# Around the expert loop of a mixture layer: fp32 router chain, early fetch of rows, p projection moved forward, last gate block by token tiles

## Chip, cores, metric

The kernel runs on one core of one Trainium2 chip. The metric is the device time of one launch in microseconds. Timed three times, the kernel before took 1843.94 us in the median (1843.38 to 1845.05).

## What is computed

256 tokens of width 1024, all in fp32. A first block (sparse attention with three branches) is untouched by the change. The second block has two layers, and the change lies in the second layer, from its output projection on:

```
h = h + mixed @ w_o                                   # (256, 1024)
f = rmsnorm(h, ffn_norm_g)
logits = f @ router_w                                 # (256, 8)
top_vals, top_idx = top_k(logits, 2)
gates = softmax(top_vals)
h = h + sum_e combine[:, e] * (silu(f @ w1[e]) * (f @ w3[e])) @ w2[e]   # 8 experts, inner width 3584
gate = sigmoid(rmsnorm(h, ple_norm_g) @ ple_gate_w)   # (256,1024) @ (1024,1024)
h = h + gate * (p @ ple_proj_w)                       # (256,256) @ (256,1024)
```

## The kernel before

**Weights.** All weights are laid out in units of 128 x 2048 fp32 words (1 MB: four k tiles of 512 columns). SyncE (`round_loads`, `load`) fetches them in the order of use into six `raw` buffers. fp32 products are made of rounded words (fp32r): ScalarE rounds a unit to its high part `whi` (`split_to`, L621), VectorE makes the low part `wlo = raw - whi` (L961), in halves of 1024 columns, into three buffers each, two units ahead of TensorE. A product of a k tile then is three matmuls of 512 columns: high x high, low x high (L1552, L1553) and high x low (L1557). Activations are turned by TensorE (`turn_rows`, L1535), split by ScalarE into `xh` with the norm's gain (`turned_high`, L637) and by VectorE into `xl` (`turned_low`, L972). The norm's factor per token (1/rms) is applied behind the products.

**Order.** Each engine runs its own queue in the order in which it is written, and semaphores tie them together. There is no planner.

**Router.** After `mix(1)`, whose last projection has two halves (`project(2)`, `project(3)`) that VectorE adds to h (`add_part`, L1342), h is turned and split like any activation. The router's weights are split too (`rws`). 32 fp32r products of 16 or 8 columns give the logits (L1988, L1990). VectorE scales them, finds the two largest by comparing all pairs (`cmpa`, `cmpb`, `sel`), and TensorE counts slots with five fp32 products (L1994 to L1998). Meanwhile VectorE makes the normed rows `tok` (L1417), ScalarE their high part `xnh`, VectorE the low part `xnl` (L1447). From the slots VectorE makes the picks of expert 0 (`make_pick`, a 0/1 matrix), TensorE gathers its tokens by 32 products of the rows with the picks (L2015, L2016), the two engines split them (`split_gathered`, L917, L1489), VectorE computes the row numbers for scattering and fetching (`make_rows`, L1467 to L1483), and the loop starts.

**Expert loop.** There are 8 rounds here, one an expert (up to 16 if an expert has over 128 tokens). GpSimd scatters the normed rows into a DRAM scratch by expert (L584), SyncE loads each next expert's rows from it. Each round leaves its output in `yo` (128 x 1024, ScalarE, L933); SyncE stores it in the next round in two halves into `y_scratch` (L502).

**Behind the loop.** The last output is stored when both halves are copied (`store`, after all six weight loads of `ple(1)`). GpSimd fetches by token, half by half, both experts' rows (`yg`, 8 indirect fetches, L591); VectorE adds them with their gates (L1518), then `ple(1)`: h is turned and split, two blocks of gate products (48 each, 12 a half unit), then two blocks of 12 products for `p @ ple_proj_w`; sigmoid on ScalarE (L664), two VectorE steps for each half of the columns (L1397, L1401), and the store of that half (L539).

The lines that set the end:

```
            for half in range(2):
                pool.wait_ge(last_stored[half], 16)
                for T in range(NT):
                    for k in range(2):
                        pool.indirect_dma_start(yg[:, k, T, half * NB:(half + 1) * NB], None,
```

## Time and profile before

| | us |
|---|---|
| median of three timed runs | 1843.94 |
| the profiled execution | 1843.26 |
| its span, first to last instruction | 1841.5 |
| expert loop, first to last product | 833.2 to 1783.1 |
| last product to end of span | 1835.7 to 1841.5 |

Mean granted clock of TensorE 0.974 of full. Busy shares: TensorE 96%, VectorE 74%, ScalarE 66%, GpSimd 1%. In all rows a time is in us from the start of the span; a bracket at the end of a timeline row gives the engine's idle time before it and whose work ended last before it started. A matmul's shown length contains its way through the array, so that matmuls of 0.39 us follow each other every 0.23. An fp32 matmul leaves two records.

### The profile page before, as it was taken

The numbers are of one execution on the slowest core, as the hardware profiler recorded it, in microseconds if no ns is written. First come the engines' busy times: TensorE is split into PE (matmuls) and PEld (weight loads), VectorE is DVE, ScalarE is ACT, GpSimd is POOL, SyncE is SP. The second block draws the span as 40 slices with busy tenths as digits, with TensorE's granted clock in tenths as the row PEclk, the third lists the DMA queues.
The fourth block names the chain that finished last, engine by engine and source line by source line (L and its number), as shares of the span: only waits on it lengthen the run. The fifth ranks groups of instructions, "written<-read, shape, count | busy, mean of one in ns | idle before, by whom it ended". The sixth has DMA issues, their size and how long they took to land.

```text
span 1841.5 us, 26253 instructions
## 1 busy us (share of the span) xinstructions
PE 1760.2 (96%) x9290; PEld 1502.9 (82%) x9290; DVE 1368.1 (74%) x1610; ACT 1215.4 (66%) x1528; POOL 22.9 (1%) x29
## 2 busy tenths in 40 slices
PE   8999978999999989989999999999999999999977
PEld 7877867989998868877888888888888888888855
DVE  4466656656665356758989899898998898989964
ACT  5555544564444355737788787887877878788763
POOL 0000000000000000001000000000000000000010
PEclk9999998999999999979999999999999999999988
DMA  9852233427845443328999999999999999999981
GB/s 332 262 177 98 81 114 120 155 98 305 348 184 207 147 170 137 138 109 323 373 372 396 351 403 383 362 406 369 379 390 354 414 369 377 390 357 407 368 306 36
DMA packets 76544, 509.54 MB, mean 277 GB/s; under 512 B 8266, under 2 KB 8394, under 8 KB 19136
## 3 DMA queue, kind: packets, MB, share of 16 engines
q1 hardware_dynamic: 70224, 484.17, 67.9%
q0 software_dynamic: 6256, 24.48, 4.4%
q8 instruction: 44, 0.72, 0.2%
q14 instruction: 20, 0.16, 0.0%
HBM read 484.51 MB, written 24.12 MB: 276 GB/s over the span
## 4 chain that ended last, share of the span: by engine, by line
PE 89%; DVE 5%; ACT 3%; issue 2%; DMA 1%; POOL 0%; POOLq 0%; ACTq 0%; DVEq 0%; SPq 0%
PE ps L1552 23%; PE ps L1553 23%; PE ps L1557 23%; PE ps L1797 4%; PE ps L1804 4%; PE ps L1798 4%; PE ps L1535 3%; DVE wlo L961 1%; DVE sg L1084 1%; ACT sg L744 1%; PE ps L1898 1%; PE ps L1619 1%; DVE xl L972 1%; ACT xh L637 1%; PE ps L1725 1%
## 5 line engine op out<-in xcount | busy, mean ns | idle before, releaser
L961 DVE TENSOR_TENSOR wlo<-raw,whi 128x1024 fp32r<-128x1024 f32 x906 | 1043.7, 1212 | 171.4 <-ACT whi L621 169.9
L621 ACT ACTIVATE whi<-raw 128x1024 fp32r<-128x1024 f32 x906 | 901.7, 1054 | 131.3 <-PE ps L1557 108.7
L1552 PE MATMUL ps<-whi,xgh 128*128 128x512 f32 x896 | 354.3, 395 | 4.6 <-ACT whi L621 4.6
L1553 PE MATMUL ps<-whi,xgl 128*128 128x512 f32 x896 | 349.6, 390 | 0.0
L1557 PE MATMUL ps<-wlo,xgh 128*128 128x512 f32 x896 | 276.8, 390 | 0.0
L1552 PE MATMUL ps<-whi,xh 128*128 128x512 f32 (+1 forms) x448 | 184.6, 413 | 23.4 <-issue 9.9
L1552 PEld LDWEIGHTS ps<-whi,xgh 128*128 128x128 f32 x896 | 168.8, 188 | 38.5 <-ACT whi L621 4.8
L1557 PEld LDWEIGHTS ps<-wlo,xgh 128*128 128x128 f32 x896 | 168.5, 188 | 35.7
L1553 PEld LDWEIGHTS ps<-whi,xgl 128*128 128x128 f32 x896 | 168.9, 188 | 33.6
L1553 PE MATMUL ps<-whi,xl 128*128 128x512 f32 (+1 forms) x448 | 179.1, 401 | 0.0
L1552 PE MATMUL ps<-whi,mTh 128*128 128x512 f32 x448 | 175.9, 393 | 0.0
L1553 PE MATMUL ps<-whi,mTl 128*128 128x512 f32 x448 | 174.4, 389 | 0.0
L1797 PE MATMUL ps<-xh,whi 128*128 128x256 f32 x640 | 157.9, 284 | 1.2 <-issue 0.7
L1798 PE MATMUL ps<-xl,whi 128*128 128x256 f32 x640 | 156.9, 283 | 0.0
L1557 PE MATMUL ps<-wlo,mTh 128*128 128x512 f32 x448 | 138.1, 389 | 0.0
L1552 PEld LDWEIGHTS ps<-whi,xh 128*128 128x128 f32 x448 | 88.3, 197 | 44.9 <-issue 22.5
L1797 PEld LDWEIGHTS ps<-xh,whi 128*128 128x128 f32 x640 | 122.7, 192 | 2.0 <-issue 1.1
L1798 PEld LDWEIGHTS ps<-xl,whi 128*128 128x128 f32 x640 | 122.8, 192 | 0.0
L1557 PE MATMUL ps<-wlo,xh 128*128 128x512 f32 (+1 forms) x448 | 121.0, 393 | 0.0
L1553 PEld LDWEIGHTS ps<-whi,xl 128*128 128x128 f32 x448 | 88.5, 198 | 17.1 <-issue 0.2
L1557 PEld LDWEIGHTS ps<-wlo,xh 128*128 128x128 f32 x448 | 86.0, 194 | 18.4
L1557 PEld LDWEIGHTS ps<-wlo,mTh 128*128 128x128 f32 x448 | 84.1, 188 | 17.7
(300 smaller groups left out, 1745.0 us busy)
## 6 DMA issues: line engine op xcount, KB each, us to landing
raw<-in_w_moe_dram SPq DMA_DIRECT2D x336, 1024.0 KB, 7.1
raw<-in_w_fixed_dram SPq DMA_DIRECT2D x112, 1024.0 KB, 5.0
tokens_scratch<-zeros POOLq DMA_DIRECT2D x1, 8704.0 KB, 44.4
y_scratch<-yo SPq DMA_DIRECT2D x18, 256.0 KB, 7.9
y_scratch<-zeros POOLq DMA_DIRECT2D x2, 2048.0 KB, 54.2
xin<-tokens_scratch SPq DMA_DIRECT2D x8, 512.0 KB, 7.4
bias_scratch<-revb POOLq DMA_DIRECT2D x1, 3072.0 KB, 38.3
bias<-bias_scratch POOLq DMA_DIRECT2D x1, 2048.0 KB, 17.1
```

Of the source, the lines that this page charges most:

```text
L621: AC(whi[:, v % SPL, c], raw[:, v % RAW, c], ACT.Copy).then_inc(high_done, 1)
L637: ins = AC(xh[:, j, :], turned_place(k, j), ACT.Copy, scale=gains[:, k, j:j + 1])
L744: ins = AC(sg[:, i % 2, r, 0:nk], sg[:, i % 2, r, 0:nk], ACT.Exp, scale=SC, bias=ast_[:, i, 1, r:r + 1], accum_out=ast_[:, i, 2, r:r + 1])
L961: V.tensor_tensor(wlo[:, v % SPL, c], raw[:, v % RAW, c], whi[:, v % SPL, c].bitcast(F32), ALU.subtract).then_inc(low_done, 1)
L972: ins = V.scalar_tensor_tensor(out=xl[:, j, :], in0=turned_place(k, j), scalar=gains[:, k, j:j + 1], in1=xh[:, j, :].bitcast(F32), op0=ALU ...
L1535: return nc.tensor.transpose(dst, src, ident if idn is None else idn)
L1552: mm(o, hi(k0 + k, T), wh[:, k, :], start=first and k == 0, stop=False)
L1553: mm(o, lo(k0 + k, T), wh[:, k, :], start=False, stop=False)
L1557: ins = mm(o, hi(k0 + k, T), wl[:, k, :], start=False, stop=last and k == nk - 1)
L1797: mm(o, w_, xh[:, kk, :], start=kk == 0 and c % 2 == 0, stop=False, skip_group_check=True)
L1798: mm(o, w_, xl[:, kk, :], start=False, stop=False, skip_group_check=True)
L1804: ins = mm(o, wl[:, k, c * P:(c + 1) * P], xh[:, kk, :], start=False, stop=kk == KD - 1, skip_group_check=True)
```

## The change

- **Router in fp32.** The turned h goes with the gain into one fp32 tile `router_x`, four column tiles by ScalarE, four by VectorE, the router's weights stay unsplit: 16 fp32 products, the first eight ahead of the transposes of h's second half, which go by token tiles. The norm's factor isn't applied to the logits but in the exponential. Squares of h are summed by halves on ScalarE as they become ready.
- **Order of work.** VectorE splits the first weight unit of the loop and the low half of p ahead of `add_part(o1 + 2)`. `p`'s high and low parts are made here, not behind the loop.
- **Selection.** Comparisons for both token tiles in one instruction; slot counts by fp32r products, the three that the slots need first. Row numbers shifted by one so that two steps fall away.
- **Gather.** The normed rows are made by ScalarE and gathered in fp32: 16 products instead of 32, in two halves, each split by itself; the first expert product waits for the first half only (the same in each round). `make_rows` goes ahead of `split_gathered(0)` on VectorE. Zeroing `yo` moves from VectorE to GpSimd.
- **Filler products** (`keep_busy`, 512 columns, results unused): 4, 5 and 3 in the router chain, 6 behind the loop.
- **First rows.** A token's lower expert is never the last one, so its rows are fetched in the last round (four fetches into `y_low`), multiplied by their gate and added to h by GpSimd. Behind the loop there are four fetches instead of eight.
- **Last stores.** Each half of the last output is stored as soon as it is copied; these stores stand ahead of the last two weight loads.
- **Last layer.** Weight order is p projection first. Its products run right behind the loop; their results are copied to `pm`. Then the gate blocks, the last one by token tiles: 24 products for tokens 0 to 127, then 24 for the others, and sigmoid, two VectorE steps and store for each.

```diff
@@ expert loop's end, SyncE
+            for half in range(2):
+                sp.wait_ge(rows_stored[half], g.at(rows_stored[half], 0))
+            sp.sem_inc(low_rows_stored, 1)
             g.post = True
             for j, unit in enumerate(after):
+                if j == 4:
+                    for half in range(2):
+                        store(half, rounds, last_stored[half])
                 load(U["ple1"] + j, unit)
-            for half in range(2):
-                store(half, rounds, last_stored[half])
...
@@ GpSimd
+            pool.wait_ge(low_rows_stored, 1)
+            for T in range(NT):
+                for half in range(2):
+                    fetch(0, T, half, y_low, low_fetched)
+            pool.wait_ge(low_fetched, 64)
+            for T in range(NT):
+                ins = pool.tensor_scalar(y_low[:, T, :], y_low[:, T, :], gk[:, 0, T:T + 1], None, ALU.mult)
+            ins.then_inc(low_scaled, 1)
+            pool.wait_ge(low_scaled, 1)
+            pool.tensor_tensor(h[:], h[:], y_low[:], ALU.add).then_inc(low_added, 1)
             for half in range(2):
                 pool.wait_ge(last_stored[half], 16)
                 for T in range(NT):
...
+                    fetch(1, T, half, y_last, y_fetched[half])
@@ ScalarE
+            def start_router(u):
+                AC(order[:], part("square")[:, 4 * P:6 * P].rearrange("p (a n) -> p a n", a=2), ACT.Copy)\
+                    .then_inc(order_set, 1)
+                split_to(u)
+                act.wait_ge(p_loaded, 32)
+                AC(p_high_1[:], pt_in[:], ACT.Copy).then_inc(ph_done, 1)
+                split_to(u + 1)
+                for half in range(2):
...
+                        ins = AC(tok[:, T, c], h[:, T, c], ACT.Square, accum_out=st[:, o:o + 1])
...
+                    for j in range(half * KU, half * KU + 2):
+                        ins = AC(router_x[:, j, :], turned_place(5, j), ACT.Copy, scale=gains[:, 5, j:j + 1])
+                    ins.then_inc(router_x_act, 1)
...
+                for T in range(NT):
+                    ins = AC(tok[:, T, :], h[:, T, :], ACT.Copy, scale=factor(T))
+                ins.then_inc(h_normed, 1)
@@ VectorE, end of mix(1)
+                    split_to(nu)
+                    dve.wait_ge(ph_done, 2)
+                    V.tensor_tensor(p_low_1[:], pt_in[:], p_high_1[:].bitcast(F32), ALU.subtract).then_inc(pl_done, 1)
+                    add_part(B["o1"] + 2)
+                    split_to(nu + 1)
+                    router_columns(0)
...
+                    add_part(B["o1"] + 3)
+                    router_columns(1)
@@ VectorE, ahead of the loop
             make_pick()
+            count_rounds()
...
-            V.memset(yo[:], 0.0).then_inc(y_copied, 2)
+            make_rows()
             split_gathered(0)
-            make_rows()
@@ VectorE, behind the loop
+            def last_ple():
+                ub, bb = U["ple1"], B["ple1"]
+                split_to(ub + 2)
+                dve.wait_ge(low_added, 1)
+                add_last(0)
+                turned_low(6, 0)
+                add_last(1)
+                split_to(ub + 3)
+                turned_low(6, 1)
+                invert_root(6)
+                split_to(ub + 5)
...
@@ TensorE
+            def keep_busy(n, u):
+                for _ in range(n):
+                    mm(ps[:, 5, :], order[:, 1, :], whi[:, u % SPL, 0:NB], start=True, stop=True)
+
+            def last_ple():
+                ub, bb = U["ple1"], B["ple1"]
+                pe.wait_ge(pl_done, 2)
+                for j in range(2):
+                    block(ub + j, bb + j, tile_of(p_high_1), tile_of(p_low_1), kt=2)
+                pe.wait_ge(high_done, g.at(high_done, 2 * (ub + 2) + 2))
+                pe.wait_ge(y_copied, g.at(y_copied, 2))
+                keep_busy(6, ub + 2)
+                turn_rows(6, 0)
+                block(ub + 2, bb + 2, *X, norm=6)
+                b = bb + 3
+                start_block(b)
+                for T in range(NT):
+                    o, rows = ps[:, pair(b) + T, :], slice(T * P, (T + 1) * P)
+                    for u in (ub + 4, ub + 5):
...
+                    ins.then_inc(gate_row, 1)
...
+            for half in range(2):
+                if half:
+                    turn_rows(5, 1)
+                    keep_busy(4, U["ffn1"])
+                pe.wait_ge(router_x_act, half + 1)
+                pe.wait_ge(router_x_dve, half + 1)
+                for k in range(half * KU, (half + 1) * KU):
+                    for T in range(NT):
+                        ins = mm(ps[:, 4, T * NE:(T + 1) * NE], router_x[:, k, T * P:(T + 1) * P], rw[:, k, :],
+                                 start=k == 0 and T == 0, stop=k == KD - 1, skip_group_check=True)
+            ins.then_inc(router_logits, 1)
+            keep_busy(5, U["ffn1"])
...
+            mm(ps[:, 1, 0:NE], order[:, 0, :], sel[:, 0, :], start=True, stop=True)
+            mm(ps[:, 1, NE:2 * NE], order[:, 0, :], sel[:, 1, :], start=True, stop=False)
+            mm(ps[:, 1, NE:2 * NE], order[:, 1, :], sel[:, 0, :], start=False, stop=True).then_inc(slots_counted, 1)
...
+            keep_busy(3, U["ffn1"])
...
+            pe.wait_ge(pick_done, 1)
+            pe.wait_ge(h_normed, 1)
+            for half in range(2):
+                for j in range(half * KU, (half + 1) * KU):
+                    for T in range(NT):
+                        ins = mm(gathered_place(j), tok[:, T, j * P:(j + 1) * P], pick[:, T, :], start=T == 0,
+                                 stop=T == 1)
                 ins.then_inc(gathered, 1)
```

## Rows read from the trace of the kernel before

**Rows 1.** The page: chain of waits by engine; one line of DMA issues.

```profile
PE 89%; DVE 5%; ACT 3%; issue 2%; DMA 1%; POOL 0%; POOLq 0%; ACTq 0%; DVEq 0%; SPq 0%
...
y_scratch<-yo SPq DMA_DIRECT2D x18, 256.0 KB, 7.9
```

**Rows 2.** Stretches: from:to, length, busy us per engine, clock, DMA share, GB/s.

```profile
675.00:680.00 5.00, 2.53 (x15) 1.72 (x13) 4.80 (x5) 0.63 (x2) 0.00 (x0) 0.98 0.55 208
680.00:685.00 5.00, 2.20 (x5) 1.82 (x6) 4.93 (x8) 2.83 (x5) 0.00 (x0) 0.50 0.00 2
810.00:812.00 2.00, 1.31 (x7) 1.32 (x7) 1.23 (x4) 1.31 (x3) 0.00 (x0) 0.50 0.78 328
833.00:837.00 4.00, 3.81 (x9) 3.03 (x10) 2.82 (x16) 1.93 (x3) 1.10 (x2) 0.52 0.00 0
1644.00:1761.00 117.00, 117.00 (x534) 96.96 (x533) 107.18 (x106) 95.27 (x106) 0.00 (x0) 1.00 0.97 379
1803.00:1809.00 6.00, 5.52 (x14) 4.26 (x15) 0.24 (x1) 0.00 (x0) 0.00 (x0) 0.50 0.01 3
```

**Rows 3.** Timeline ahead of the loop: start, length, engine, line, operation, shapes.

```profile
798.08 1.41 DVE L1342 SCALAR_TENSOR_TENSOR h<-ps,st,h 128x512 f32<-128x512 f32 x2 [2.50 <-PE ps L1557]
...
804.79 1.40 DVE L1342 SCALAR_TENSOR_TENSOR h<-ps,st,h 128x512 f32<-128x512 f32 x2
...
810.69 0.38 PE L1988 MATMUL ps<-rws,xh 128*128 128x16 f32 x1 [1.67 <-DVE xl L972]
...
814.30 0.36 DVE L1422 TENSOR_SCALAR lg<-ps,st 128x8 f32<-128x8 f32 x2 [1.31 <-PE ps L1990]
...
816.80 0.17 DVE L1440 TENSOR_SCALAR sel<-sel 128x16 f32<-128x16 f32 x1
...
820.93 0.48 DVE L1461 TENSOR_SCALAR pick<-con,slot 128x128 fp32r<-128x128 f32 x2
...
828.60 2.17 ACT L917 ACTIVATE xgh<-ps,con 128x128 fp32r<-128x128 f32 x8 [10.77 <-PE ps L2016]
...
830.80 2.16 DVE L1489 SCALAR_TENSOR_TENSOR xgl<-ps,con,xgh 128x128 fp32r<-128x128 f32 x8 [7.23 <-ACT xgh L917]
...
833.19 0.79 PE L1552 MATMUL ps<-whi,xgh 128*128 128x512 f32 x1 [4.63 <-ACT whi L621]
...
834.87 0.19 DVE L1483 TENSOR_REDUCE gk<-rowf 128x4 f32<-128x32 f32 x1
```

**Rows 4.** Timeline behind the loop.

```profile
1781.36 0.58 ACT L933 ACTIVATE yo<-ps 128x512 f32<-128x512 f32 x1
...
1783.88 0.83 SPq L502 DMA_DIRECT2D y_scratch<-yo  x2
1786.16 1.00 POOL L591 DMA_INDIRECT yg<-y_scratch,rowy  x1 [944.59 <-DMA y_scratch<-yo]
...
1803.48 0.79 PE L1552 MATMUL ps<-whi,xh 128*128 128x512 f32 x1 [4.84 <-DVE xl L972]
...
1835.79 1.23 DVE L1397 TENSOR_TENSOR pm<-ps,pg 128x1024 f32<-128x1024 f32 x1 [0.24 <-PE ps L1557]
```

**Rows 5.** Chain of waits, pieces in order of time: start, us, what.

```profile
780.70 0.88 PE ps L1898 x6
...
793.41 1.68 PE ps L1921 x16
...
1795.03 3.63 DMA yg<-y_scratch,rowy
...
1829.35 0.91 PE ps L1557 x4
```

**Rows 6.** Timelines of GpSimd, SyncE's queue and VectorE.

```profile
432.62 0.95 POOL L571 MEMSET zeros<- 128x1024 f32 x1 [40.30 <-ACT hTh L789]
...
1744.67 16.10 SPq L494 DMA_DIRECT2D raw<-in_w_moe_dram  x7
...
1765.59 18.24 DVE L961 TENSOR_TENSOR wlo<-raw,whi 128x1024 fp32r<-128x1024 f32 x16
```

More of the change, by code:

```diff
@@ L160, in part @@
             return con[:, a:a + n]
-        ident, ntri, nones, negm, stri, ones, iota = (part("square")[:, i * P:(i + 1) * P] for i in range(7))
+        ident, ntri, nones, negm, stri, ones, place_ = (part("square")[:, i * P:(i + 1) * P] for i in range(7))
         keep = stri
@@ L427, in through @@
             def through(self, b):
-                end = block_end[b] if not (self.post and b >= B["ple1"]) else U["ple1"] + ple_end[b - B["ple1"]]
+                end = block_end[b] if not (self.post and b >= B["ple1"]) else U["ple1"] + last_ple_end[b - B["ple1"]]
                 return self.at(half_used, 2 * end)
@@ L975, in turned_low, with router_columns @@
                 ins.then_inc(xl_done, 1)
+            def router_columns(half):
+                dve.wait_ge(h_turned, 10 + half - 1)
+                for j in range(half * KU + 2, (half + 1) * KU):
+                    ins = V.tensor_scalar(router_x[:, j, :], turned_place(5, j), gains[:, 5, j:j + 1], None, ALU.mult)
+                ins.then_inc(router_x_dve, 1)
             for half in range(2):
@@ L1423, in _ @@
-            step(ins)
-            for T in range(NT):
-                ins = V.scalar_tensor_tensor(out=lg[:, T], in0=ps[:, 0, (2 * T + 1) * NE:(2 * T + 2) * NE],
-                                             scalar=factor(T), in1=lg[:, T], op0=ALU.mult, op1=ALU.add)
-            step(ins)
+            step(V.tensor_copy(lg[:].rearrange("p t e -> p (t e)"), ps[:, 4, 0:NT * NE]))
             other = lg[:].unsqueeze(2).broadcast_to([P, NT, NE, NE])
             own = lg[:].unsqueeze(3).broadcast_to([P, NT, NE, NE])
-            for T in range(NT):
-                V.tensor_tensor(cmpa[:, T], other[:, T], own[:, T], ALU.is_gt)
-                ins = V.tensor_tensor(cmpb[:, T], other[:, T], own[:, T], ALU.is_equal)
@@ L1433, in _ @@
-            step(ins)
-            for T in range(NT):
-                ins = V.tensor_tensor(cmpb[:, T], cmpb[:, T], tril8.rearrange("p (a b) -> p a b", a=NE), ALU.mult)
-            step(ins)
+            lower = tril8.rearrange("p (a b) -> p a b", a=NE).unsqueeze(1).broadcast_to([P, NT, NE, NE])
+            V.tensor_tensor(cmpa[:], other, own, ALU.is_gt)
+            step(V.tensor_tensor(cmpb[:], other, own, ALU.is_equal))
+            step(V.tensor_tensor(cmpb[:], cmpb[:], lower, ALU.mult))
@@ new lines, in _ @@
+            chosen = sel[:].bitcast(F32)
+            step(V.tensor_reduce(st[:, 12:14], lg[:], AX, ALU.max))
+            V.tensor_tensor(gw[:], lg[:], st[:, 12:14].unsqueeze(2).broadcast_to([P, NT, NE]), ALU.subtract)\
+                .then_inc(logit_shift, 1)
+            dve.wait_ge(sel_done, 1)
+            dve.wait_ge(slots_counted, 1)
+            step(V.scalar_tensor_tensor(out=slot[:], in0=ps[:, 1, 0:NT * NE].rearrange("p (t e) -> p t e", t=NT),
+                                        scalar=1.0, in1=chosen, op0=ALU.add, op1=ALU.mult))
@@ L1470, in make_rows @@
                                             scalar=float(P), in1=low, op0=ALU.mult, op1=ALU.add))
-                V.scalar_tensor_tensor(out=high, in0=low, scalar=1.0, in1=sel[:], op0=ALU.add, op1=ALU.mult)
-                step(V.scalar_tensor_tensor(out=low, in0=low, scalar=float(2 * NE * P), in1=sel[:], op0=ALU.subtract,
-                                            op1=ALU.mult))
+                V.tensor_tensor(high, low, chosen, ALU.mult)
+                step(V.scalar_tensor_tensor(out=low, in0=low, scalar=float((2 * NE + 1) * P + 1), in1=chosen,
+                                            op0=ALU.subtract, op1=ALU.mult))
@@ L1512, in _ @@
             g.r = rounds
-            for half in range(2):
-                c = slice(half * NB, (half + 1) * NB)
-                dve.wait_ge(y_fetched[half], 64)
-                for k in range(2):
-                    for T in range(NT):
-                        ins = V.scalar_tensor_tensor(out=h[:, T, c], in0=yg[:, k, T, c], scalar=gk[:, k, T:T + 1],
-                                                     in1=h[:, T, c], op0=ALU.mult, op1=ALU.add)
-                    if k == 0:
-                        step(ins)
-                ins.then_inc(h_combined, 1)
-            dve.wait_ge(h_combined, 2)
             g.split = U["ffn1"] + 2
             g.post = True
-            ple(1)
+            last_ple()
         @block_.tensor
@@ L1839, in turn_hidden, with second_half @@
                     ins.then_inc(hidden_turned, 1)
+                def second_half():
+                    pe.wait_ge(gather_low, g.at(gather_low, 2))
                 for f in range(NFB):
-                    block(ub + 4 * f, bb + 2 * f, *x, nt=1)
+                    block(ub + 4 * f, bb + 2 * f, *x, nt=1, between=second_half if f == 0 else None)
                     if f:
@@ L2003, in turn_tokens @@
+            mm(ps[:, 0, 0:NE], order[:, 1, :], sel[:, 1, :], start=False, stop=True).then_inc(slots_counted, 1)
+            keep_busy(3, U["ffn1"])
             def turn_tokens():
```

356 lines of the change are left out of this document (206 added, 150 removed).

## Prediction

> **What bounds the kernel now.** I read the chain of waits first, on the page: 89% of the span is TensorE, 5% VectorE, 3% ScalarE [rows 1]. Then the table by stretches: in a round of the expert loop TensorE is busy for all 117.0 of 117 us at clock 1.00, VectorE for 107.2 [rows 2]. The change leaves the number of products in the loop alone, so the eight rounds should cost what they cost now. What is left are the stretches before and behind the loop, and there I read the timeline, looking at the brackets that name an idle time. Before the loop TensorE does no weight product from 804.3 (VectorE's last add starts behind it, at 804.79) to 833.2, and its clock is down from 810 on (0.50) and still low until about 836.8, 3.6 us into the products (0.52 in 833 to 837) [rows 2, 3]. Behind the loop the last product ends at 1783.1 and the first of the next block starts at 1803.5: store, eight indirect fetches on one queue, adds, transposes, split [rows 4].
>
> **Part 1, the router chain.** A schedule step by step, each time against the one of before.
> Start: VectorE now splits weight unit 0 (2 x 1.2 us, and ScalarE reaches it 0.4 later) and the low half of p (0.7) before its first add, which starts at 799.8 and not at 798.08 [rows 3]. TensorE is busy with the first half of its last projection until 800.5, so of the 1.7 us it sees 0.7: the last projection ends at 805.05, not 804.3.
> fp32 router: the trace has fp32 products whose moving side is narrow: 16 records (8 products) in 1.68 us, 0.21 each; and wide ones: 6 records with 512 columns in 0.88, so 0.22 for 128 columns [rows 5]. The 16 router products thus cost 3.4 us, as many as the 32 of before at full clock. Their first half (1.7) now stands ahead of the transposes of the second half: these start at 806.8 although the first add is ready at 805.8. Eight transposes 0.9, columns copied by two engines at once 0.9 to 1.0, second half 1.7: logits at 810.75, against 814.30 [rows 3]. Gained 3.5, of which about 1.7 is the second half at full clock.
> Logits to selection: 2.67 us before (814.30 to 816.97 [rows 3]); with one copy for four scalings and whole 128-element comparisons I count 1.9: 812.65.
> Selection to picks: before 4.4 us, to 821.4. In it were a 2.28 us low part of the normed rows on VectorE, five fp32 products at low clock, and seven small steps of 0.2 [rows 3]. Now three products (0.35), 0.4 until they are seen, one step 0.2, picks 0.5, some 0.2 of handoffs: 814.3. The normed rows are made by ScalarE (root 809.5, two copies of 1.07) by 811.9, which is early enough; zeroing the output tile goes to the idle GpSimd (0.95 for its like [rows 6]) and costs nothing.
> Gather: 7.1 us before (to 828.60 [rows 3]); now 16 fp32 products x 0.22 = 3.5, in halves at 816.1 and 817.9.
> Split: ScalarE's first half is ready at 817.5. But VectorE now does the rounds (0.8), the gate weights (1.0 plus handoffs) and all row numbers first; these took 2.1 (from 832.95, end of the split, to 835.06 [rows 3]) and end at about 818.3. That queue is late next, and not TensorE. First half of its split: half of 2.16, so 819.4, and the first expert product starts at 819.7, against 833.19: gained 13.5. The second half is ready at 820.5 and its unit is needed 2.7 us after the start: hidden.
> Clock: if filler products hold it, the first 3.6 us of expert products, now at half speed, cost half: another 1.7. The fillers (12 of 512 columns, 0.23 each) stand in waits for other engines and I cost them at nothing; at low clock the last three would push the gather by about 1. Part 1: **15.2 us**.
>
> **Part 2, behind the loop.**
> The lower expert's rows: SP has issued the last round's last weight load at 1760.8 (1744.67 + 16.10 [rows 6]) and then releases GpSimd. Four fetches of 1.27 each (eight issues from 1786.16 to 1795.03 [rows 4, 5]) end at 1766, land within some 8 us while the DMA engines are full (the y store takes 7.9 there [rows 1]): 1774. Then GpSimd multiplies 2 x 1024 columns and adds 2048. The trace has no GpSimd arithmetic. Lower bound: 4096 columns at the rate of its memset (0.95 per 1024 [rows 6]) are 3.8 us; upper bound three times that, 11.4, since it reads where the memset only writes. I take 7, so it is done at 1781, before the 1784.3 at which it is wanted; with the upper bound it is 1 us late.
> Does this hold up VectorE? From 1765.6 on it makes low parts back to back, 16 in the 18.24 us listed, 1.14 each, where TensorE takes 1.36 for each; it runs about 5 us ahead [rows 6]. If it stopped for the whole arithmetic, 7 us, less what it regains, some 1 us would come out at TensorE; with 11.4 about 5. I take 0.5.
> The Trainium skill, "SBUF — State Buffer", section "Who interferes with whom", says of this that a VectorE instruction with two SBUF inputs and a GpSimd instruction that reads SBUF exclude each other for the whole instruction; the split of weights is such an instruction. No run here shows it yet. By the Trainium skill, "GPSIMD Engine Reference", section "3.1 Elementwise — side-by-side cycle accounting", an add of 2048 fp32 columns takes 4.5 us on GpSimd; with 2.2 for the multiplications the sum would be 6.7, all of it taken from VectorE. This goes into the second rival.
> Last rows: the first half of the output is now stored by itself: copied by 1781.94, on its way at 1782.05; store to GpSimd took 2.3 (1783.88 to 1786.16), so 1784.3 [rows 4]. Two fetches instead of four per half: the second is issued at 1785.6 and lands 3.63 later [rows 5], 1789.2. New is that two 1 MB weight loads are now queued behind the stores and run at that time: between 0 and 4.3 (7.9 less 3.6) more; I take 1. Two adds of 0.75: h at 1791.7. From the end of such adds to the next product, over transposes, high and low parts, before the router: 806.2 to 810.69, 4.5 us [rows 3]. First gate product 1796.2, against 1803.48 [rows 4]. The second half's rows land by 1793 and are added behind the first low part: hidden.
> p projection: 24 products of 0.2275 (0.91 for four [rows 5]) = 5.5 us go into the wait, from 1783.1 to 1788.6, and fillers until 1790. What had covered them was nothing; now VectorE and ScalarE have that time too.
> Clock: after the fillers TensorE has only transposes for 6 us. The same happened at 676 to 682.8: 0.98 up to 680, then 0.50 [rows 2]. So I expect the clock to fall and the first 5.3 us to run at half speed as they do now (0.50 in 1803 to 1809 [rows 2]).
> From the first gate product to the last product of all are 32.2 us now (1803.48 to 1835.7, just ahead of VectorE's 1835.79 [rows 4]); less 5.5 is 26.7, so the end is at 1822.9. The order by token tiles changes no count: 48 products again. Weight units 4 and 5 are loaded at about 1784.5, split by 1810 and needed at 1808 to 1811, so not late by the schedule, but with little to spare.
> Behind the last product: now 5.8 us: two VectorE steps of 1.23 from 1835.79, and 3.2 from their end to the span's end at 1841.5 [rows 4]. With a tile of 128 tokens: sigmoid 0.64 and handoffs 0.3, two steps of 0.62, 0.2, and 2.6 for half the bytes: 5.0. End at 1827.9 instead of 1841.5. Part 2: **13.6 us**, less 0.5 for VectorE: 13.1.
>
> **Sum.** 15.2 + 13.1 = 28.3. The profiled execution took 1843.3 (span 1841.5 and 1.8 around it); 1843.3 - 28.3 = 1815.0. The median of the timed runs is 0.7 above it, so I say 1815.5.
>
> **Rivals.**
> A. The clock falls before the gather all the same. For it: between 805 and 810.6 only the four fillers are dense, and at 810 it fell before. Against: no stretch without dense work is longer than 2.7 us, and it held in 675 to 680 for 3.5 us without any. Then the second half of the router takes 3.4, the gather 7, the first products run slowly: the loop starts at 823.2, part 1 is worth 10.0. Time 1820.7.
> B. GpSimd and VectorE exclude each other, and the arithmetic waits for gaps or takes the upper bound. The last round loses up to 5 at TensorE, or the fetches of the last rows, queued behind the arithmetic on GpSimd, go out 3 to 5 late. Time 1820 (1818 to 1824). Against it: ten free microseconds before 1784.
> C. Better than I say: the clock survives the wait behind the loop (2.6) and the loads don't disturb the fetches (1). Time 1812. Against: 676 to 683.
> D. Slower than before. GpSimd's arithmetic is of another order. Everything of the tail waits for it: the last fetches, the adds, the gate. It starts at 1774 and has 10 us; beyond this each microsecond is one of the span. The other gains are spent when it lasts 38 us, ten times the memset's rate; at 45 us the time would be 1850. For it speaks only that the trace has no such operation.
> E. The change doesn't do what it says: the rows of the lower expert aren't ready in the last round because SP comes to its signal late, or the split chain on VectorE (rows first) holds the loop. Then each part keeps about half: 1829.
>
> **Chances.** Forecast 0.50, A 0.18, B 0.13, C 0.09, E 0.06, D 0.04. The forecast's own range is 1812.5 to 1819. For 8 in 10 I take 1810.5 to 1826: it holds A, B, most of C. About 0.2% (3.7 us) is what a measurement of this kernel can tell from no change. Faster by more 0.95, within it 0.01, slower 0.04.
>
> **What would show it.** In the profile after: first product on the gathered tokens at about 820 and clock 1.00 there; the 16 gather products 0.22 apart; GpSimd's arithmetic between 1760 and 1770 of the new span (13 to 15 us earlier than here) and no idle TensorE in the last round; first gate product some 13 us behind the loop's last product, with the p products between; last product to end 5 us. I am wrong if TensorE idles in a round, if the loads of gate units 4 and 5 end a wait, or if the gather products are 0.43 apart.

## The result and the profile after

The changed kernel takes 1829.84 us (median, 1829.60 to 1830.73); the kernel before, timed beside it, 1844.49. The ratio is 0.992, 95% interval 0.9907 to 0.9932. Faster, as predicted, but by 14.7 us instead of 28.3. The predicted time was 1815.5, and 1829.84 lies outside both the forecast's own range (to 1819) and the wider one (to 1826). The profiled span is 1828.2 us, 13.3 less than before.

Part 1 came as drawn. Timeline of the changed kernel ahead of the loop (start, length, engine, line, operation, as in [rows 3]):

```profile
803.72 1.41 DVE L1436 SCALAR_TENSOR_TENSOR h<-ps,st,h 128x512 f32<-128x512 f32 x2 [0.81 <-PE ps L1669]
...
809.32 0.17 DVE L1553 COPY lg<-ps 128x16 f32<-128x16 f32 x1 [1.43 <-PE ps L2142]
...
811.03 0.17 DVE L1563 TENSOR_SCALAR sel<-rank 128x16 fp32r<-128x16 f32 x1
...
812.16 0.48 DVE L1576 TENSOR_SCALAR pick<-con,slot 128x128 f32<-128x128 f32 x2
...
813.54 4.47 PE L2170 MATMUL ps<-pick,tok 128*128 128x128 f32 x32
...
817.45 1.13 DVE L1613 SCALAR_TENSOR_TENSOR xgl<-ps,con,xgh 128x128 fp32r<-128x128 f32 x4 [1.07 <-ACT xgh L1006]
...
818.80 0.49 PE L1664 MATMUL ps<-whi,xgh 128*128 128x512 f32 x1 [0.79 <-DVE xgl L1613]
```

Logits at 809.3 (predicted 810.75), first expert product at 818.80 (predicted 819.7, before 833.19). The first product has its full-clock duration, 0.49, where it had 0.79 [rows 3].

Part 2 did not. The last expert output is copied out at 1767.02, 16.1 us earlier than before (1783.12), yet the span is only 13.3 shorter. GpSimd's timeline behind that point, with all it did there:

```profile
1751.70 13.18 POOL L613 DMA_INDIRECT y_low<-y_scratch,rowy  x1 [929.91 <-SPq L552]
1765.18 0.97 POOL L613 DMA_INDIRECT y_low<-y_scratch,rowy  x1 [0.30 <-issue]
1766.45 0.99 POOL L613 DMA_INDIRECT y_low<-y_scratch,rowy  x1 [0.30 <-issue]
1767.74 0.95 POOL L613 DMA_INDIRECT y_low<-y_scratch,rowy  x1 [0.31 <-issue]
1775.66 5.68 POOL L624 TENSOR_SCALAR y_low<-y_low,gk 128x1024 f32<-128x1024 f32 x2 [6.97 <-DMA y_low<-y_scratch,rowy]
1781.43 4.49 POOL L627 TENSOR_TENSOR h<-h,y_low 128x2048 f32<-128x2048 f32 x1
1786.08 1.02 POOL L613 DMA_INDIRECT y_last<-y_scratch,rowy  x1 [0.15 <-issue]
```

The fetch of the last expert's rows (last line) has no wait of its own left: 0.15 idle, released by "issue", that is by its place in the queue. The store that it needs had been issued at 1766.01. The chain of waits of the changed kernel says the same, read downward in time:

```profile
1745.75 5.56 issue
1751.70 13.18 POOL y_low L613
1767.74 7.83 DMA y_low<-y_scratch,rowy
1775.66 5.68 POOL y_low L624 x2
1781.40 4.53 POOLq L140
1787.41 3.55 DMA y_last<-y_scratch,rowy
1792.52 1.99 PE ps L1647 x8
```

Before, this chain went from the last copy over store and fetch to the adds [rows 4, 5]. Now it begins in the middle of the last round and runs through GpSimd: the work meant to lie beside the loop has become the path. The stretches of the changed kernel (columns as in [rows 2]) show no wait in the last round, the clock half down during the gather, and the hole in front of the last gate blocks:

```profile
806.00:812.00 6.00, 5.08 (x33) 4.04 (x31) 3.06 (x13) 5.28 (x9) 0.95 (x1) 0.97 0.17 66
812.00:819.00 7.00, 6.21 (x38) 5.74 (x38) 4.99 (x31) 2.10 (x9) 1.77 (x2) 0.78 0.17 68
1650.00:1760.00 110.00, 110.00 (x504) 91.17 (x503) 100.92 (x101) 90.51 (x104) 8.30 (x1) 1.00 0.97 373
1774.00:1786.00 12.00, 0.00 (x0) 0.00 (x0) 0.00 (x0) 0.00 (x0) 10.18 (x3) 0.65 0.23 95
1786.00:1800.00 14.00, 3.94 (x13) 3.16 (x14) 5.28 (x9) 3.46 (x6) 3.88 (x4) 0.50 0.28 75
```

From 1774 to 1786 only GpSimd works, 10.2 of 12 us. In the first 14 us after it the clock stands at 0.50.

**The measure used below.** Kernels that share all code up to the router still reach it up to 6 us apart (the last add starts at 803.72 in the changed kernel, at 810.06 in best below), so small changes of the tail drown in the total. I therefore take the *tail* from each profile: from the start of the copy of the last rows' second half (`yo`, second of two) to the end of the span. The two starts, before and changed:

```profile
1783.12 0.60 ACT L933 ACTIVATE yo<-ps 128x512 f32<-128x512 f32 x1 [1.18 <-PE ps L1557]
```

```profile
1767.02 0.60 ACT L1021 ACTIVATE yo<-ps 128x512 f32<-128x512 f32 x1 [1.18 <-issue]
```

Before 1841.5 - 1783.12 = 58.4; changed 1828.2 - 1767.02 = 61.2. The loop itself, first expert product to that copy, is 949.9 before and 948.2 in the changed kernel (1.7 for products no longer at half the clock, as predicted). It is steady: 948.2 in all the kernels below but one (early_pool). A tail is read from one trace for each kernel. low_dve and probe, which differ only in two small GpSimd instructions, have 50.1 and 50.6, so I read nothing from a difference of half a microsecond.

### The profile page after: what moved, and what is told of

Read it like the earlier page. It is cut to its first block, busy times and chain, and to the rows that moved or that the text cites. A ratio compares the mean times of both kernels' runs of the same rounds, so it can differ in the third digit from the quotient of the medians.

```text
span 1828.2 us, 26305 instructions
## 1 busy us (share of the span) xinstructions
PE 1754.7 (96%) x9303; PEld 1497.1 (82%) x9303; DVE 1362.0 (74%) x1591; ACT 1221.8 (67%) x1533; POOL 45.4 (2%) x33
## 4 chain that ended last, share of the span: by engine, by line
PE 87%; DVE 5%; ACT 3%; issue 2%; POOL 1%; DMA 1%; POOLq 0%; SPq 0%; DVEq 0%; ACTq 0%
PE ps L1664 22%; PE ps L1665 22%; PE ps L1669 22%; PE ps L1918 4%; PE ps L1925 4%; PE ps L1919 4%; PE ps L1647 3%; DVE wlo L1049 2%; DVE sg L1178 1%; POOL y_low L613 1%; ACT sg L816 1%; PE ps L2022 1%; PE ps L1740 1%; ACT whi L658 1%; ACT xh L674 0%
## 5 line engine op out<-in xcount | busy, mean ns | idle before, releaser
L1664 PE MATMUL ps<-whi,xh 128*128 128x512 f32 (+1 forms) x432 | 177.7, 413 | 22.1 <-issue 10.0
L1665 PE MATMUL ps<-whi,xl 128*128 128x512 f32 (+1 forms) x432 | 172.1, 400 | 0.0
L1669 PE MATMUL ps<-wlo,xh 128*128 128x512 f32 (+1 forms) x432 | 116.6, 393 | 0.0
L1664 PEld LDWEIGHTS ps<-whi,mTh 128*128 128x128 f32 x448 | 84.1, 188 | 17.0
## 6 DMA issues: line engine op xcount, KB each, us to landing
bias<-bias_scratch POOLq DMA_DIRECT2D x1, 2048.0 KB, 17.4
```

The source lines that it names most:

```text
L1664: mm(o, hi(k0 + k, T), wh[:, k, :], start=first and k == 0, stop=False)
L1665: mm(o, lo(k0 + k, T), wh[:, k, :], start=False, stop=False)
L1669: ins = mm(o, hi(k0 + k, T), wl[:, k, :], start=False, stop=last and k == nk - 1)
```

## The experiments

Theory: the gain of part 2 went into a new chain on GpSimd that stands in its queue ahead of the last rows' fetches: a signal 7 us late, a first fetch 12 us too long, 10 us of arithmetic. The diffs below show each edit's main lines. Rivals: the last rows' own store and landing set the time; or part 1 was worth less than it looks and part 2 did gain.

### Part 1 alone: front_only

```diff
-        return proj + gate if i else gate + proj
+        return gate + proj
-            pool.wait_ge(low_rows_stored, 1)
...
+            for half in range(2):
+                pool.wait_ge(last_stored[half], 16)
+                for T in range(NT):
+                    for k in range(2):
+                        fetch(k, T, half, y_last if k else y_low, y_fetched[half])
```

> The changed kernel with the router part as changed, and behind the expert loop the order of the kernel before (six weight units in the old order and the stores behind them, all eight row fetches behind the stores, both experts' rows added by VectorE, gate blocks ahead of the p projection). Theory: the router part alone is worth what the profile of the changed kernel shows at the loop's end, 1783.12 to 1767.02, so 16.1 us of 1844.5: 1828.4 us. Then the whole part behind the loop gives nothing (1829.8 measured for both together, so +1.4). Rival: the router part is worth only the 14.4 us by which the first expert product came earlier, 1830.1, and the other 1.7 us in the loop belong to the new order behind it; then the part behind the loop gives about nothing too. If it is above 1833, the part behind the loop did help and the router part was worth less than its trace says.

Measured: 1827.63 us (1826.66 to 1833.03), ratio 0.9913 (0.9884 to 0.9941). Tail 1824.9 - 1767.42 = 57.5. So part 1 alone has all of the gain (18.3 us by the medians here, 16 by its trace). The intervals of the two ratios overlap, so the timed runs don't show whether part 2 gives or costs anything. By the tails of the two traces, part 2 as built costs 3.7 us (61.2 against 57.5). The rival that part 2 did gain falls. The loop takes 948.2 here too, so the 1.7 us gained in it belong to part 1, against the rival in the expectation.

### Who does the adds: low_dve

```diff
-            pool.wait_ge(low_fetched, 64)
-            for T in range(NT):
-                ins = pool.tensor_scalar(y_low[:, T, :], y_low[:, T, :], gk[:, 0, T:T + 1], None, ALU.mult)
-            ...
-            pool.tensor_tensor(h[:], h[:], y_low[:], ALU.add).then_inc(low_added, 1)
+                dve.wait_ge(low_fetched, 64)
+                for T in range(NT):
+                    ins = V.scalar_tensor_tensor(out=h[:, T, :], in0=y_low[:, T, :], scalar=gk[:, 0, T:T + 1],
+                                                 in1=h[:, T, :], op0=ALU.mult, op1=ALU.add)
```

> The changed kernel, with the low expert's rows scaled and added to h by two VectorE instructions of 1024 columns instead of GpSimd's three. Theory (the last rows' fetches queue behind GpSimd's arithmetic): GpSimd is free at 1775.7 instead of 1785.9, so the last rows' fetches and all behind them come 10.2 us earlier: 1819.6 us, and down to 1817 if TensorE's clock no longer falls in the shorter wait. The first fetch stays at 13 us, its landing at 7 to 8. Rival 1 (the arithmetic excludes VectorE and was not itself on the path): less than 2 us, 1828. Rival 2 (the last rows' store or landing sets the time): the fetches go out earlier but land only a little earlier, 1826.

Measured: 1821.02 us (1819.19 to 1822.76), ratio 0.9864 (0.9839 to 0.9889). The time expected was 1819.6. Tail 1821.0 - 1770.90 = 50.1: 11.1 us less than the changed kernel, the 10.2 of arithmetic and a bit of what follows. The two adds on VectorE take 2.48 us for what took GpSimd 10.2. GpSimd's timeline of this kernel, and VectorE's adds:

```profile
1755.33 13.42 POOL L613 DMA_INDIRECT y_low<-y_scratch,rowy  x1 [929.64 <-SPq L552]
...
1774.07 1.59 POOL L613 DMA_INDIRECT y_last<-y_scratch,rowy  x1 [1.50 <-DMA y_scratch<-yo]
...
1778.83 2.48 DVE L1521 SCALAR_TENSOR_TENSOR h<-y_low,gk,h 128x1024 f32<-128x1024 f32 x2 [3.99 <-DMA y_low<-y_scratch,rowy]
```

The first fetch is as long as ever (13.42), but the last rows' fetch now waits for its own store (1.50, "DMA y_scratch<-yo"). Both rivals said under 4 us and fall. And with the arithmetic gone, neither the late signal nor the long fetch costs much.

### The fetch in the last round: early_pool and early_dve

```diff
-            pool.wait_ge(low_rows_stored, 1)
+            for half in range(2):
+                pool.wait_ge(rows_stored[half], 16 * NE)
```

SyncE's own two waits and its signal behind the loop are dropped. early_dve has the edit of low_dve as well.

> The changed kernel, but GpSimd itself waits for the eighth store of rows (a constant that holds for the 8 rounds of this input) and not for SyncE's word at its loop's end; the arithmetic stays on GpSimd, and so falls into the last round. Theory: the late signal (7 us) and the blocked fetch (12 us) then lie beside the loop, the last rows are fetched when their store has landed, about 1769.4 instead of 1786.1: 16.7 us, 1813 us. If VectorE's gapless stream is what shut the first fetch out, that fetch lasts until VectorE has its first gap, in the last round too, and VectorE's operations run longer beside GpSimd's arithmetic (7 to 10 us of it), which TensorE may feel: up to 7 us, 1820. If it was cold code or a busy queue, the first fetch is long whatever VectorE does, or short (1 us) because the queue is quieter, and the loop is not longer. Rival: the last rows' chain is bound by something else (store, landing): over 1822.

> As early_pool, with the low expert's rows added by VectorE behind the loop (2 instructions, about 2.7 us, while the last rows are still under way). Theory: 1813 us as well, 1 to 3 us under early_pool if GpSimd's arithmetic beside the loop cost the loop anything. Rival: 1819.6, as low_dve, if only the arithmetic's place mattered and not the fetches'.

Measured: early_pool 1823.58 us (1818.50 to 1824.65), ratio 0.9883 (0.9859 to 0.9908), tail 1816.7 - 1768.27 = 48.4; early_dve 1818.60 us (1817.22 to 1819.61), ratio 0.9856 (0.9832 to 0.9880), tail 1815.4 - 1767.99 = 47.4. Both are under low_dve's tail, by 1.7 and 2.7, but not by the 6 or 7 expected. By the medians early_pool is no better than low_dve (1821.02) and early_dve only slightly, and the intervals of all three ratios overlap. The theory's 1813 us is missed by 10 and 6; the measured times lie near those of the two rivals (over 1822, and 1819.6). GpSimd's arithmetic in early_pool, beside VectorE's stream:

```profile
1657.43 1.90 POOL L610 DMA_INDIRECT y_low<-y_scratch,rowy  x1 [835.67 <-DMA y_scratch<-yo]
...
1672.56 11.94 POOL L622 TENSOR_SCALAR y_low<-y_low,gk 128x1024 f32<-128x1024 f32 x2 [8.13 <-DMA y_low<-y_scratch,rowy]
1684.59 5.46 POOL L625 TENSOR_TENSOR h<-h,y_low 128x2048 f32<-128x2048 f32 x1
```

and VectorE in that time:

```profile
1672.67 4.62 DVE L1047 TENSOR_TENSOR wlo<-raw,whi 128x1024 fp32r<-128x1024 f32 x4
...
1684.36 9.03 DVE L1047 TENSOR_TENSOR wlo<-raw,whi 128x1024 fp32r<-128x1024 f32 x4
```

17.4 us instead of 10.2, and VectorE's four splits 9.03 instead of 4.62 while GpSimd adds: each engine waits for the other. TensorE felt it once (0.91 idle at 1691, waiting for `wlo`), and the loop is 949.5, where every other kernel with the new router part has 948.2. So even hidden, this arithmetic costs 1.3 us. A first fetch after 836 us of waiting took 1.90 here, so cold code is not what made it 13.

Why not 1813? In early_dve the store and fetches go out early, the rows come late:

```profile
1769.06 0.86 SPq L514 DMA_DIRECT2D raw<-in_w_fixed_dram  x2
...
1769.22 0.95 POOL L610 DMA_INDIRECT y_last<-y_scratch,rowy  x1 [103.82 <-DMA y_scratch<-yo]
...
1778.16 1.41 DVE L1510 SCALAR_TENSOR_TENSOR h<-y_last,gk,h 128x512 f32<-128x512 f32 x2 [3.84 <-DMA y_last<-y_scratch,rowy]
```

8.9 us from first fetch to add, where the prediction has 5.9. The half's last fetch, issued at 1770.48, has 7.7 us to the add; in front_only it is 3.7 (1774.30 to 1778.02). The difference between the two is what the change queued behind the stores: two 1 MB weight loads, issued from 1769.06.

### Loads and rows: loads_first, best, rows_first

loads_first is low_dve, and best is early_dve, with the loads ahead of the stores; rows_first is early_dve with the last two loads behind the rows.

```diff
# loads_first, best
             for j, unit in enumerate(after):
-                if j == 4:
-                    for half in range(2):
-                        store(half, rounds, last_stored[half])
                 load(U["ple1"] + j, unit)
+            for half in range(2):
+                store(half, rounds, last_stored[half])
# rows_first
                         store(half, rounds, last_stored[half])
+                    sp.wait_ge(y_fetched[0], 32)
```

> low_dve with one thing put back: SyncE issues all six weight loads before the two stores of the last rows, as the kernel before did. Theory: in low_dve and early_dve two 1 MB loads went out 2.1 us after the first store (at 1771.98 and 1769.06), and the rows fetched behind them landed 6 to 7 us after their issue, against 2.8 to 3.6 us in front_only, where nothing else was under way; with the loads ahead the last rows' first half comes about 3 us earlier, so 1818 us. Rival 1: the store now goes out later than it did, because the sixth load waits for its buffer, and eats the gain: 1821 us. Rival 2: GpSimd is not ready before 1773 because of the long first fetch of the low expert's rows (13.4 us) and the three behind it, so only 1 us is left of it: 1820 us.

> early_dve (GpSimd fetches the low expert's rows in the last round, on its own wait; VectorE adds them behind the loop) with the loads ahead of the stores. Theory: the last rows are fetched at 1769.2 and land at about 1774.0 instead of 1778.1 (early_dve), so 4 us less than early_dve: 1814.5 us, and up to 2 us less again where TensorE's wait is now short enough for its clock to stay up. Rival: the landing does not depend on the two loads: 1818.5 us as early_dve.

> early_dve with the last two weight loads held back until the first half of the last rows has landed (SyncE waits for y_fetched[0]); in best the same two loads, put ahead of the stores, made the first store land 4.9 us after its issue instead of 2.2. The measure is the stretch from the start of the copy of the last rows' second half to the end of the span, since the time ahead of the expert loop differs by up to 6 us between executions that share all of that code: 58.4 us before, 61.2 in the changed kernel, 47.4 in early_dve, 46.4 in best. Theory (store, fetch and loads share the DMA engines, and the rows are what TensorE waits for): store as in early_dve, landing of the first half at about 1774.2 on its scale instead of 1778.1, first transposes 4 us earlier: 43.5 us, and 1814.5 us in all. Rival: the held loads are late for the last gate block, 47 us or more.

Measured: loads_first 1820.53 us (1820.12 to 1824.22; tail 1818.4 - 1768.77 = 49.6, low_dve 50.1); best 1820.96 us (1817.93 to 1821.54; tail 1819.7 - 1773.33 = 46.4, early_dve 47.4). Little, and not the 3 and 4 us expected. Timelines of SyncE's queue and of GpSimd in best:

```profile
1772.32 1.98 SPq L522 DMA_DIRECT2D y_scratch<-yo  x2
...
1777.24 0.95 POOL L609 DMA_INDIRECT y_last<-y_scratch,rowy  x1 [106.50 <-DMA y_scratch<-yo]
```

From store to fetch it is now 4.9 us (7.0 in loads_first, 1767.75 to 1774.71), in early_dve 2.25: the loads that no longer sit on the rows sit on the store. (The median of best is above early_dve's. In the two profiled executions that difference lies ahead of the loop, in code that both share: the products start at 825.1 instead of 819.8. For the other executions it isn't known.) rows_first takes both off: 1815.51 us (1813.68 to 1816.38), ratio 0.9833 (0.9816 to 0.9849), tail 1811.9 - 1768.54 = 43.4, expected 43.5:

```profile
1774.90 1.41 DVE L1511 SCALAR_TENSOR_TENSOR h<-y_last,gk,h 128x512 f32<-128x512 f32 x2
1776.37 0.86 PEld L1645 LDWEIGHTS ps<-con,h 128*128 128x128 f32 x8 [1.33 <-DVE h L1511]
```

The adds start 6.4 us behind the second copy instead of 10.2, with no wait for a DMA in front of them; the held loads are in time.

### What shuts the fetch out: gaps and probe

```diff
# gaps: in VectorE's split, last 16 of each round
+                            V.memset(st[:, 60:61], 0.0).then_inc(gap_made, 1)
+                            dve.wait_ge(gap_made, g.at(gap_made, 2 * w + half + 1))
# probe: on GpSimd, behind the signal
+            pool.memset(y_low[:, 0, 0:64], 1.0).then_inc(low_scaled, 1)
+            pool.wait_ge(low_scaled, 1)
+            pool.tensor_scalar(y_low[:, 1, 0:64], y_low[:, 0, 0:64], 2.0, None, ALU.mult).then_inc(low_scaled, 1)
+            pool.wait_ge(low_scaled, 2)
```

> low_dve, but in every round VectorE waits for a tiny write of its own behind each of its last 16 splits of weights, so that it stands still for a moment after each; nothing else differs, and the first fetch of the low expert's rows is issued by SyncE's word as in low_dve. Theory (the first fetch is shut out as long as VectorE goes from one instruction to the next without a gap): it now lasts 1 to 2.3 us instead of 13.4, and the four fetches end by about 1762. Rival 1 (busy queues or the weight loads make it long): still 10 us or more. Rival 2 (GpSimd's code is cold when it has waited 930 us): unchanged too, but early_pool's 1.9 us after 836 us of waiting speak against it.

> low_dve with two small GpSimd instructions between SyncE's word and the first fetch: a memset of 64 columns and a multiplication of 64 columns that reads what it wrote. Theory (GpSimd gets at SBUF only when VectorE leaves a gap): the memset or the multiplication is the long one, 10 us or more, ends about 0.1 to 0.9 us after VectorE's first gap, and the first fetch behind it takes 1 to 2 us. Rival (it is the fetch's own descriptors that are held up): both small instructions take under 0.5 us, and the fetch still lasts to VectorE's first gap, over 10 us.

Both were run once. First probe, then gaps, GpSimd's timeline behind SyncE's word:

```profile
1752.25 0.15 POOL L619 MEMSET y_low<- 128x64 f32 x1 [929.50 <-SPq L552]
1752.50 12.74 POOL L621 TENSOR_SCALAR y_low<-y_low 128x64 f32<-128x64 f32 x1
1765.51 1.67 POOL L613 DMA_INDIRECT y_low<-y_scratch,rowy  x1 [0.27 <-POOL y_low L621]
```

```profile
1757.86 1.00 POOL L614 DMA_INDIRECT y_low<-y_scratch,rowy  x1 [930.06 <-SPq L553]
1759.16 1.02 POOL L614 DMA_INDIRECT y_low<-y_scratch,rowy  x1 [0.30 <-issue]
```

Both rivals of gaps fall, busy queues and cold code, and so does that of probe. A GpSimd instruction that only writes 64 columns takes 0.15 us in the middle of VectorE's stream; one that reads 64 columns takes 12.74. So neither the fetch's queue nor its code holds it up; a plain read of SBUF by GpSimd is held up just the same. The stretches of probe up to and behind the point where it is let in show VectorE at 12.99 of 13.00 us, then with air:

```profile
1752.00:1765.00 13.00, 13.00 (x59) 10.78 (x58) 12.99 (x12) 10.96 (x11) 12.65 (x2) 1.00 0.69 245
...
1765.00:1768.00 3.00, 3.00 (x15) 2.49 (x14) 2.45 (x2) 1.55 (x2) 2.42 (x3) 1.00 0.15 14
```

With a short stop behind each split (VectorE busy 8.9 of 10 us in gaps), the same fetch at the same place takes 1.00. The Trainium skill, "SBUF — State Buffer", section "Who interferes with whom", gives the rule: a VectorE instruction with two SBUF inputs contends with a GpSimd instruction that reads SBUF, and not with one that only writes it. The trace agrees, 12.74 against 0.15. The section infers that descriptor generation needs the write side and so is left alone by such a stream; here the measurement decides otherwise, 13.18 us for an indirect fetch. That a fetch is held up because it takes its row numbers from SBUF, which is a read, is argued from these two runs and not shown by itself.

Its price is small once the arithmetic is gone: gaps has a tail of 1820.3 - 1772.99 = 47.3 (1822.15 us in all, its products starting 6 us late as in best), low_dve 50.1, so 2.8 us. That is also all that early_dve gains over low_dve: with the fetch let in, SyncE's late word costs nothing that the tails show. Each of these figures is from one run. probe took 1820.45 us (tail 50.6, as low_dve).

### Clock and token tiles: rows_fill, gate_whole, front_no_fill

```diff
# rows_fill, on rows_first
-                keep_busy(6, ub + 2)
+                keep_busy(9, ub + 2)
                 turn_rows(6, 0)
+                start_block(bb + 2)
+                for _ in range(13):
+                    mm(ps[:, pair(bb + 2), :], order[:, 1, :], whi[:, (ub + 2) % SPL, 0:NB], start=True, stop=True)
                 block(ub + 2, bb + 2, *X, norm=6)
# gate_whole, on rows_first
-                for T in range(NT):
-                    o, rows = ps[:, pair(b) + T, :], slice(T * P, (T + 1) * P)
...
+                block(ub + 4, bb + 3, *X)
```

front_no_fill is the changed kernel less `keep_busy(4, ...)`, `(5, ...)` and `(3, ...)` of the router part.

> rows_first with 9 instead of 6 matrix products without use ahead of the transposes, and 13 more behind the first transposes, where TensorE stands still for 3.5 us in every version (1781.60 in early_dve). Theory: TensorE's granted clock stays at 1.00 through the wait for h; the gate products that ran at half the clock (in early_dve the clock was 0.50 to about 1789) take half as long: 3 us less than rows_first, 40.5 us of the stretch behind the copy and 1811.5 us. Rival: the clock falls all the same, or the fillers end late and hold the gate products up: rows_first's time or up to 2 us more.

> rows_first with the last gate block as one block again (whole sigmoid, whole product and sum of 1024 columns, one output store), to price the change's work by token tiles. By the rows of before the end behind the last product is 1.0 of ScalarE, 1.2 and 1.2 of VectorE in place of 0.7, 0.7 and 0.7, so the stretch is 1.5 to 2 us longer than rows_first's. Rival: the token tiles win nothing, because the first tile's work was hidden anyway and the output store sets the end: under 0.5 us.

> The changed kernel without the 12 products without use in the router part (the 6 behind the loop stay). Measured from the last product of the output projection (803.72 in the changed kernel) to the first expert product (818.80), 15.1 us. Theory: without them the clock is at half for the gather and the logits; the 32 records of the gather take about 6.6 us instead of 4.5 and the logits and transposes a little longer, 17.5 to 18.5 us, and the first expert products up to 4 us at half the clock, so 20 us in all by the loop's end. Rival: the clock would not have fallen, 15.1 us.

rows_fill: **1811.70 us** (1810.96 to 1815.88), ratio 0.9818 (0.9799 to 0.9837), tail 1809.2 - 1768.16 = 41.0, the fastest of all and faster than both kernels (the changed one has 0.992, 0.9907 to 0.9932). The stretch behind the transposes, rows_first and then rows_fill:

```profile
1776.00:1784.00 8.00, 4.09 (x15) 3.28 (x16) 4.00 (x8) 3.57 (x6) 0.00 (x0) 0.70 0.75 310
```

```profile
1776.00:1784.00 8.00, 7.48 (x38) 6.00 (x39) 4.22 (x8) 3.58 (x6) 0.00 (x0) 1.00 0.68 284
```

Granted clock 1.00 instead of 0.70; 2.4 us of tail for 16 useless products. (Every kernel with early_dve's wait holds a constant for 8 rounds and is not general as it stands.)

gate_whole, one run, 1818.88 us: tail 1817.1 - 1771.40 = 45.7, 2.3 more than rows_first: the token tiles are worth a little more than the 1.5 to 2 expected. Storing the last output by halves and the p projection ahead of the gate have no run of their own. front_no_fill, one run, 1832.41 us: first expert product 820.18 - 803.89 = 16.3 us behind the last add instead of 15.1, last copy 1768.38, so 1.2 us later in all. I had expected 5. Stretches of front_no_fill, then of the changed kernel:

```profile
812.00:815.00 3.00, 2.37 (x10) 2.31 (x11) 1.97 (x14) 0.49 (x2) 0.00 (x0) 0.50 0.45 175
815.00:818.00 3.00, 3.00 (x16) 3.00 (x15) 2.23 (x17) 0.36 (x2) 0.00 (x0) 0.50 0.00 0
818.00:821.00 3.00, 2.85 (x19) 2.53 (x18) 1.12 (x4) 1.73 (x8) 2.34 (x3) 0.87 0.43 175
```

```profile
812.00:815.00 3.00, 3.00 (x12) 2.71 (x12) 2.62 (x17) 0.01 (x1) 0.00 (x0) 0.50 0.25 94
815.00:818.00 3.00, 3.00 (x27) 2.83 (x25) 1.79 (x14) 1.14 (x4) 1.05 (x1) 0.99 0.00 0
```

The fillers bring the clock back some 3 us sooner, within the gather. Without them the gather itself brings it back before the expert products, so these lose nothing: 1.2 us is all that the fillers of part 1 earn.

## Why the prediction was wrong

**Part 1 (predicted 15.2, measured about 16) was right**, step for step within 2 us: logits 1.4 early, first product 0.9 early, 1.7 at the head of the loop. Two details were off. VectorE's row numbers, named as "late next", were not: its split waited 1.07 us for ScalarE. And the gather took 4.5 us and not 3.5, since the clock was at 0.50 up to 815 in spite of the fillers, as rival A had it; it came back during the gather, so A's other costs did not arise.

**Part 2 (predicted 13.1, measured -2.8) failed in its first paragraph, "the lower expert's rows".** On the changed kernel's scale (16.1 us earlier) the schedule ran:

- *Last weight load issued "at 1760.8", "and then releases GpSimd"*: 1744.7 here, as planned, but the word came at 1751.70, 7.0 us late. The chain books 5.56 of it as "issue", between SyncE's branch on the number of rounds (L546, at 1745.7) and its next instruction (L551, at 1751.3). In between, at 1749.5 to 1749.8, lies one packet of the DMA queue that loads instructions; whether SyncE waited for it no run shows.
- *"Four fetches of 1.27 each"*, 5.1 us: they took 17.0, the first alone 13.18. +11.9. I did cite the rule of exclusion, but applied it to the arithmetic only: a fetch reads SBUF too.
- *Landing 8*: 7.0 from the end of the last issue. -1.0.
- *Arithmetic "I take 7"*: 10.25. +3.3. It lay inside my bounds (3.8 to 11.4), near the upper end. The add of 2048 columns took 4.49, as the 4.5 that the prediction names for it; the two multiplications took 5.68 where it had 2.2.

Together 21 us late: ready at 1785.9 instead of 1764.9, wanted at 1768.2. So the last rows' fetches went out 17.9 us late. The rest of the tail was priced well: fetch to adds 5.0 (5.9), adds to first gate product 7.0 (6.0), 25.6 to the last product (26.7), 4.6 behind it (5.0). 17.9 - 0.9 + 1.0 - 1.1 - 0.4 = 16.5 against the plan, less 1.4 (0.9 more gained in front, and the 0.5 booked for VectorE, which TensorE never lost): the 15 us that are missing.

**What decided** was less each delay than the order: the arithmetic stood in GpSimd's queue ahead of fetches that did not need it. low_dve keeps the late word and the long fetch, takes only the arithmetic away, and has 11.1 of the 16.5 back; early_dve 2.7 more. The schedule asked whether the low rows were ready in time and gave the queue behind them a sentence ("go out 3 to 5 late") in rival B. B named the mechanism, exclusion and late fetches behind the arithmetic, at 0.13 and at less than a third of its size (3 to 5 late, measured 17.9); its "ten free microseconds" were eaten before the arithmetic began. The time came out beside rival E's 1829, which had the late signal, but not as E had it: part 1 kept all and part 2 nothing.

**Two terms in part 2 were guesses that the runs now price.** The loads behind the stores: I took 1 of a range of 0 to 4.3. In the changed kernel they ran while GpSimd was busy and cost the last rows nothing; once the fetches are on time (early_dve against rows_first) they cost 4.0. "The clock will fall behind the fillers" was right (0.50 in 1786 to 1800); holding it is worth 2.4, near the 2.6 of rival C.

## What to carry to other kernels

Work moved off the path onto an idle engine must be followed to what stands behind it in that engine's queue; if something urgent does, the moved work is on the path again, with all its delays. GpSimd is idle but not free: while VectorE streams instructions with two SBUF inputs, a GpSimd instruction that reads SBUF, and a fetch with row numbers too, can wait for a gap (12.74 and 13.18 us here), and VectorE in turn can wait for GpSimd (9.03 instead of 4.62). Where a small transfer ends the path, keep large loads off the DMA engines both ahead of its store and behind it; give the loads a wait on the rows.

## What the runs showed of the hardware

- A GpSimd instruction (a fetch, in probe a read of 64 columns) was shut out beyond the end of the current VectorE instruction: in the changed kernel over ten such ends in a row, 1.135 us apart. It took 12.74 to 13.74 us in four kernels (changed, low_dve, loads_first, probe; 13.18, 13.42, 13.74, 12.74), and 1.00 with a stop behind each. In early_pool, with VectorE also going from one split to the next, a fetch came through in 1.90. What tells these two apart stays open; no run was made for it.
- Both sides pay: GpSimd's multiplications 11.94 instead of 5.68, its add 5.46 instead of 4.49, VectorE's four splits 9.03 instead of 4.62.
- SyncE's word behind its loop came 7.0 us after the issue of its last load of the loop (1744.7 to 1751.70), and 6.5 to 6.8 in low_dve, loads_first and probe. What takes that time stays open.
- Executions with the same code ahead of the router reach the first expert product between 818.8 and 825.1 us; from there to the last copy it is 948.20 to 948.23 us in every kernel with the new router part but early_pool.
